# Value pages of a hybrid decoder step: sums of groups of four pages, on TensorE in column strips and on VectorE

## The reference

```python
t_inv = inverse(eye + L)                 # L: strictly lower part of (k*beta) k^T * decay
u = t_inv @ v_beta
w = t_inv @ (k_beta * exp(g))
def step(S, xs):
    v_new = u_c - w_c @ S
    o = q_c @ S + attn_c @ v_new
    S = S * exp(gl) + k_c^T @ v_new
```

```python
v_past = v_pool[page_table].reshape(db, past, HA, DVA)      # 8 x 16 pages of 128 x (4 heads x 128)
a = p[:, :, 0] - lam * p[:, :, 1]                           # weights, one for each position and head
out = einsum('bhqk,bkhe->bqhe', a, v)
```

## Time and profile before

| | us |
|---|---|
| median of 3 runs (lowest to highest) | 2703.61 (2703.09 to 2705.79) |
| the profiled execution | 2701.74 |
| its span, which the rows below divide | 2699.8 |
| TensorE busy, over the span | 2622.1 (97%) |
| VectorE busy, over the span | 1614.7 (60%) |
| ScalarE, GpSimd busy | 1142.6, 1346.6 |
| L1396, 360 of its operations | 106.9 |

### The profile page before, as it was taken

One profiled execution on the slowest core, in us unless ns is written; L12 is line 12 of the kernel. 1 busy time (PEld: TensorE's weight loads), 2 busy tenths in 40 slices (PEclk: granted clock), 3 DMA queues, 4 the chain that ended last, 5 costly groups with the idle time before them and its releaser, 6 DMA issues.

```text
span 2699.8 us, 46857 instructions
## 1 busy us (share of the span) xinstructions
PE 2622.1 (97%) x17069; PEld 2408.8 (89%) x17069; DVE 1614.7 (60%) x3290; ACT 1142.6 (42%) x1771; POOL 1346.6 (50%) x613
## 2 busy tenths in 40 slices
PE   8999999978899999999999999999999999999998
PEld 5886666667766899999999999999999999999998
DVE  4227768889977343333337885378863788634323
ACT  2228739954423343334333434344343433444433
POOL 0210015610000666667666676676766767666663
PEclk9999999988899999999999999999999999999999
DMA  5220057634585444444444444454444444444553
GB/s 182 68 95 9 17 173 222 195 103 133 155 251 156 134 143 141 137 139 138 139 140 141 134 140 130 138 147 133 140 132 144 132 142 140 134 132 141 149 156 95
DMA packets 457194, 369.01 MB, mean 137 GB/s; under 512 B 15501, under 2 KB 400114, under 8 KB 456732
## 3 DMA queue, kind: packets, MB, share of 16 engines
q1 hardware_dynamic: 444846, 347.05, 43.6%
q0 software_dynamic: 2992, 12.26, 1.5%
q10 hardware_dynamic: 9174, 7.22, 0.9%
HBM read 351.17 MB, written 17.14 MB: 136 GB/s over the span
## 4 chain that ended last, share of the span: by engine, by line
PE 67%; DVE 2%; ACT 1%; issue 1%; DMA 0%; SPq 0%; POOL 0%; DVEq 0%; ACTq 0%
PE bank L2867 21%; PE bank L2869 21%; PE bank L2868 21%; PE bank L2359 3%; DVE tmp L2735 1%; DVE bank L3448 1%; ACT tmp L2727 1%; DMA big<-in_cache_attn_v 0%; PE bank L2743 0%; PE bank L3651 0%; PE bank L2379 0%; SPq L1128 0%; DVE hh L3405 0%; DVE hl L3406 0%; PE bank L1759 0%
## 5 line engine op out<-in xcount | busy, mean ns | idle before, releaser
L3326 POOL TENSOR_TENSOR wl<-wring,wh 128x1024 fp32r<-128x1024 f32 x466 | 1137.4, 2456 | 589.3 <-ACT wh L3083 588.9
L2867 PE MATMUL bank<-xh,wh 128*128 128x344 f32 x2688 | 862.2, 321 | 0.3 <-POOL wl L3326 0.3
L2869 PE MATMUL bank<-xh,wl 128*128 128x344 f32 x2688 | 858.4, 319 | 0.0
L2868 PE MATMUL bank<-xl,wh 128*128 128x344 f32 x2688 | 856.8, 319 | 0.0
L3083 ACT ACTIVATE wh<-wring 128x1024 fp32r<-128x1024 f32 x466 | 484.1, 1055 | 766.3 <-PE bank L2869 642.4
L2867 PEld LDWEIGHTS bank<-xh,wh 128*128 128x128 f32 x2688 | 505.6, 188 | 1.8 <-POOL wl L3326 0.6
L2868 PEld LDWEIGHTS bank<-xl,wh 128*128 128x128 f32 x2688 | 504.0, 188 | 1.2
L2869 PEld LDWEIGHTS bank<-xh,wl 128*128 128x128 f32 x2688 | 505.0, 188 | 0.0
L3404 DVE TENSOR_TENSOR bank<-bank,gates_tmp 128x344 f32<-128x344 f32 x132 | 69.1, 524 | 512.0 <-PE bank L2869 420.0
L3448 DVE SCALAR_TENSOR_TENSOR bank<-big,vec,bank 128x344 f32<-128x344 f32 (+1 forms) x696 | 354.5, 572 | 0.5
L2867 PE MATMUL bank<-hh,wh 128*128 128x344 f32 x1040 | 334.2, 321 | 3.2 <-DVE hl L3406 3.2
(11 more groups left out here) (441 smaller groups left out, 3182.9 us busy)
## 6 DMA issues: line engine op xcount, KB each, us to landing
wring<-in_ffn_w_down SPq DMA_DIRECT2D x132, 512.0 KB, 3.6
wring<-in_ffn_w_gate SPq DMA_DIRECT2D x131, 512.0 KB, 3.9
wring<-in_ffn_w_up SPq DMA_DIRECT2D x131, 512.0 KB, 3.9
wring<-in_conv_w_pw SPq DMA_DIRECT2D x72, 512.0 KB, 3.8
big<-in_cache_attn_k SPq DMA_DIRECT2D x128, 256.0 KB, 3.0
big<-in_cache_attn_v SPq DMA_DIRECT2D x128, 256.0 KB, 2.9
wring<-in_w_in SPq DMA_DIRECT2D x20, 512.0 KB, 4.0
park<-res_a SPq DMA_DIRECT2D x1, 4128.0 KB, 12.9
```

Of the source, the lines that this page charges most:

```text
L2867: pe.matmul(bank_out, h, mh, start=(n == 0), stop=False)
L2868: pe.matmul(bank_out, h, ml, start=False, stop=False)
L2869: mm = pe.matmul(bank_out, l, mh, start=False, stop=(n == len(terms) - 1))
L3326: pool.tensor_tensor(wl[s % 6][:, :], raw_w[s % WQ] if raw is None else raw, wh[s % 6][:, :].bitcast(F32), ALU.subtract).then_inc(w_cut, 1)
```

## The change

In each turn the 12 pages are now three groups of four.

- The first two groups go to TensorE (`page_group`). Four products of 128x32 weights by a whole page of 128x512 write to the four strips of 32 partitions of one PSUM bank (bank 5 for the first group, bank 6 for the second). Of the 32 weight columns, four are the heads' weights for that page; the others give rows that nothing reads. VectorE then copies or adds the bank to `strip_sum` in SBUF (`group_copy`, semaphore `group_in`).
- The third group stays on VectorE, pages 0 and 1 late in turn k, pages 2 and 3 early in turn k + 1. After the last turn two such pages follow.
- `page_column` adds, for the batches in the loop, four products of `strip_sum` with the columns of `fold`, which pick and sum the four strips.
- `keys_queries` goes ahead of `turn_values` on TensorE, and their marks in `set_at` change places.
- TensorE gets waits: ahead of the first group for the last VectorE page and for bank 5 (`attn_done`), ahead of the second for bank 6 (`k_scaled`), ahead of `values_new` and `outputs` for the group copies. Pages are still used in order, so a group waits for all pages before it.

The core of the diff:

```diff
+        def page_group(pe, g, n):
+            b, at = g * STRIPS // PG, g * STRIPS
+            pe.wait_ge(vpage_used, 8 + at)
...
+            for q in range(STRIPS):
+                pp, u = (at + q) % PG // 2, q % 2
+                w = aw_flat[:, (at + q) * H:(at + q) * H + 32]
+                mm = pe.matmul(bank[32 * q:32 * (q + 1), n, :], w, ring[:, pp % 4, u, :], start=True, stop=True)
+            mm.then_inc(vpage_used, STRIPS)
+
+        def group_copy(dve, g, n):
+            b = g * STRIPS // PG
+            dve.wait_ge(vpage_used, 8 + STRIPS * (g + 1))
+            d, src = strip_sum[b % 2].rearrange("p h e -> p (h e)"), bank[:, n, :]
+            if g == first_of(b, True):
...
+                dve.tensor_copy(d, src).then_inc(group_in, 1)
+            else:
+                dve.wait_ge(group_in, pe_groups(g))
+                dve.tensor_tensor(d, d, src, ALU.add).then_inc(group_in, 1)
...
             for h in range(H):
-                mm = pe.matmul(bank[:, n, h:h + 1], pacc[b][:, h, :], ones[:, 0:1], start=True, stop=True)
+                mm = pe.matmul(bank[:, n, h:h + 1], pacc[b][:, h, :], ones[:, 0:1], start=True, stop=not strips)
+                if strips:
+                    mm = pe.matmul(bank[:, n, h:h + 1], strip_sum[b % 2][:, h, :], fold[:, h:h + 1], start=False, stop=True)
...
                 left(k - 1, 3)
+                keys_queries(k)
                 turn_values(k)
-                keys_queries(k)
...
                 turn_keys(k)
+                if k < NB:
+                    pe.wait_ge(attn_done, k + 1)
+                else:
+                    pe.wait_ge(vn_copied, k - 1)
+                page_group(pe, 3 * (k - 1), 5)
                 left(k, 0)
...
+                pe.wait_ge(group_in, 2 * k - 1)
                 values_new(k - 1)
                 left(k, 2)
+                pe.wait_ge(group_in, 2 * k)
                 outputs(k - 1)
```

More of the change, by code:

```diff
@@ L1383, in page_sum @@
                 dve.wait_ge(page_in[pp % 4], b * 64 + (512 + 32 * (pp // 4 + 1)))
-            if g % PG == 0 and 2 <= b < 6:
+            first = g == STRIPS * first_of(b, False)
+            if first and 2 <= b < 6:
                 dve.wait_ge(samp_full, b - 1)
@@ L1392, in page_sum @@
                 w, d = aw_flat[:, at:at + 1], pacc[b][:, h, :]
-                if g % PG == 0:
+                if first:
                     last = dve.tensor_scalar(d, v, w, None, ALU.mult)
@@ L1610, in build, with on_pe, pe_groups, first_of @@
         samp_full, sacc_done = sem("samp_full"), sem("sacc_done")
-        PAGES = (0,) + 8 * (12,)
-        LATE = sum(PAGES)
+        STRIPS = 4
+        GROUPS = 3 * NB
+        LATE = STRIPS * GROUPS
         SAMPLE_AT = {2: 0, 4: 1, 5: 2, 6: 3, 8: 4}
-        KK, VT, QK, KT = 1, 2, 3, 4
+        group_in = sem("group_in")
+        strip_sum = [flat(16 * TT, H, P), flat(16 * TT + 512, H, P)]
+        def on_pe(g):
+            return g < GROUPS and g % 3 < 2
+        def pe_groups(g):
+            return sum(on_pe(n) for n in range(g))
+        def first_of(b, pe):
+            return next(g for g in range(b * PG // STRIPS, (b + 1) * PG // STRIPS) if on_pe(g) == pe)
+        KK, QK, VT, KT = 1, 2, 3, 4
         def set_at(c, what):
@@ L1813, in page_column @@
             pe.wait_ge(vpage_used, 8 + PG * (b + 1))
+            strips = pe_groups((b + 1) * PG // STRIPS) if b < LATE // PG else 0
+            if strips:
+                pe.wait_ge(group_in, strips)
             for h in range(H):
-                mm = pe.matmul(bank[:, n, h:h + 1], pacc[b][:, h, :], ones[:, 0:1], start=True, stop=True)
+                mm = pe.matmul(bank[:, n, h:h + 1], pacc[b][:, h, :], ones[:, 0:1], start=True, stop=not strips)
+                if strips:
+                    mm = pe.matmul(bank[:, n, h:h + 1], strip_sum[b % 2][:, h, :], fold[:, h:h + 1], start=False, stop=True)
             mm.then_inc(samp_full, 1)
+        def page_group(pe, g, n):
[3 more added lines that the diff above has]
+                pp, u = (at + q) % PG // 2, q % 2
+                if u == 0:
+                    pe.wait_ge(page_in[pp % 4], b * 64 + 512 + 32 * (pp // 4 + 1))
+            for q in range(STRIPS):
+                pp, u = (at + q) % PG // 2, q % 2
+                w = aw_flat[:, (at + q) * H:(at + q) * H + 32]
[6 more added lines that the diff above has]
+            if g == first_of(b, True):
+                if b >= 2:
+                    dve.wait_ge(samp_full, b - 1)
+                else:
+                    dve.wait_ge(bias_io, 64)
+                dve.tensor_copy(d, src).then_inc(group_in, 1)
+            else:
+                dve.wait_ge(group_in, pe_groups(g))
+                dve.tensor_tensor(d, d, src, ALU.add).then_inc(group_in, 1)
         def page_column_in(dve, b, n):
@@ L2032, in chunk_pe @@
                     on_sum(pe, 2, ON_BANK[2])
+                    pe.wait_ge(oc_copied, k - 1)
+                else:
+                    pe.wait_ge(k_scaled, k + 1)
+                page_group(pe, 3 * (k - 1) + 1, 6)
                 right_turned(k - 1, 5)
@@ L2174, in chunk_dve @@
         def chunk_dve(dve, step):
-            def page(k, n):
-                if n < PAGES[k]:
-                    page_sum(dve, sum(PAGES[:k]) + n)
             def decays(c):
@@ L2331, in chunk_dve @@
                 join_turned(k, 2)
-                page(k, 11)
+                page(k, 1)
                 lower(k + 1)
-                page(k, 12)
                 if k in SAMPLE_AT:
                     page_column_in(dve, SAMPLE_AT[k], 2 * ((k + 1) % 2))
+            page(NB, 2)
+            page(NB, 3)
         vecf = vec[:].rearrange("p k v -> p (k v)")
```

20 lines of the change are left out of this document (9 added, 11 removed).

## The result

The changed kernel takes 2711.66 us (median of 10 runs, 2709.89 to 2717.63) against 2703.54 us (10 runs, 2701.22 to 2706.78) of the kernel before on the same chip: ratio 1.0031, 95% interval 1.0021 to 1.0040. It is slower by 8 us, where 2 us faster was forecast. The profiled execution took 2712.34 us, 2710.5 of them its span.

The account below looks back on a forecast made before the run. Inside a turn no engine was simply full: waits between TensorE and VectorE, then the falling clock, set it. -7.7 us at full clock plus 5.6 for clock falls gave -2.1, from 2703.6 to 2701.5 us; range 2692 to 2716.

Parts of the forecast that it names:

- Step 4: Ahead of the level-3 join: VectorE's page 2 adds 1.05 us, level-4 product 6.56 us after level 3, not 5.51.
- Step 6: New values to turn's end: turn of 23.4 us, or 24.9 with a column sum of 1.9 us on the path.
- Step 8: Granted clock early in the turn: falls in two of six turns, 2.5 us each, 0.6 in the last: +5.6 us.
- Step 7: Full-clock sum: six turns -5.6 us, last turn 19.3 against 20.5, first -0.3, after the loop -0.6; in all -7.7.
- Step 1: Strip products on TensorE: a group of four takes 1.05 us, upper bound 3.4, lower 0.85.
- the rival of serial strips: Both groups of each turn: strips run one after another, 2.35 us more for each of 16 groups, 2735 us; chance 0.13.
- Step 2: VectorE's work per turn: eight pages leave, two copies or adds come, giving 7 to 8 us of room.
- Step 3: Turn's start up to the key-state product, 4.43 us after level 3: moving the key-query products ahead gains nothing.
- Step 5: First group to new values: join waits of 1.23 and 1.36 us go, new values 0.83 us earlier.
- The rival of late pages: Second group's pages land late, costing a microsecond or two only at 728 to 745; near no change; chance 0.03.
- The rival "the clock falls in every turn": Clock falls at the wait for the level-3 join in every turn: +8.3 us, 2712 us; chance 0.12.

Follow-up runs that it names:

- filled: Changed kernel plus four unread 128x128 products on TensorE behind the key-state product in each turn but the last: 2706.24 us, 1.0011 of the kernel before.
- page_behind: Changed kernel with VectorE's page 2 moved back behind the level-3 join: 2704.09 us, 0.9998 of the kernel before.
- product_later: Changed kernel with GpSimd's product of the decayed queries held until VectorE has summed its four pages: 2706.89 us, 1.0009 of the kernel before.
- no_strip_sums: Changed kernel without the four products that add the strip sums into a column sum: 2701.72 us, 0.9996 of the kernel before.
- queries_back: Changed kernel with the key-query products behind the turned values again: 2710.33 us, 1.0029 of the kernel before.
- spread: Changed kernel with VectorE's four pages moved, three ahead of the level-2 join, one behind the lower triangle: 2686.61 us, 0.9938 of the kernel before.
- spread_queries_back: Changed kernel with VectorE's pages moved to its idle places and key-query products behind the turned values again: 2686.59 us, 0.9938 of the kernel before.

## Why the prediction was wrong

The forecast was 2701.5 us, and 2711.66 came: inside the range of 2692 to 2716, with the wrong sign. By the forecast's steps turns 2 to 8 add up to 146.4 + 19.3 + 5.6 = 171.3 us; the profile has 181.14. Three steps failed: the size of the hole (4), the cost of a column sum (6) and, most of all, the number of the clock's falls (8). Of the 9.8 us between the two sums:

- **Step 4, the hole: 2 us of work, taken for 1.** The mechanism was right: page 2 ahead of the join holds up the level-4 product, with nothing to hide it. Its size, 1.05 us, came from a page that ran alone. This page runs beside GpSimd's product, 2.11 us instead of 1.14. With the hole at t = 7.48 instead of 6.56, and steps 5 and 6 half a microsecond better than worked out, a full-clock turn without a column sum is 23.86 us (`filled`) and not 23.4.
- **Step 6, the column sum.** 1.9 us were worked out for its own time and 1.5 for the turn; it costs the turn 1.78 (25.64 less 23.86). With the point above, the six turns at full clock are 4 x 25.64 + 2 x 23.86 = 150.3 us and not 146.4: **3.9 us**.
- **Step 8, the clock: the larger part.** Falls were expected in two of six turns, 5.0 us; they came in five, once twice as long and once with a second fall behind the column sum. The six turns took 159.6 us, 9.3 more than at full clock: **4.3 us**. The number was the guess between rivals that the text called it. The price of 2.5 us was that of a turn with twice the low clock (2.6 measured, in turns 4 and 5); a single fall cost 1.4 to 1.5, so two such turns would have been 2.9 us and not 5.0, and the number was off by more than the 4.3 us show. The place was nearly right: t = 6.2 to 9.0, in the hole or up to 1.5 us behind it, where 6 to 7 was forecast. That the hole is to blame is shown from two sides: `filled` and `page_behind` have waits of 1.0 to 1.6 us there too, but more work between them, and no fall; in `product_later` the wait is 0.9 us with nothing put in, and the falls stay.
- **Step 7, the last turn.** 19.3 us at full clock plus 0.6 were expected, 21.58 came: **1.7 us**. The outputs wait for the second group's add, as was forecast, for 1.56 us, and run at half clock behind it. `product_later` has the same wait and a last turn of 19.89 us at full clock (below), and so has `no_strip_sums` with its wait of 2.46. So the 19.3 was 0.6 too low, and the clock took 1.7 instead of 0.6: with the last turn it explains 5.4 of the 9.8 us.

```profile
772.39 0.79 PE L2024 MATMUL bank<-res_b,state 128*128 128x128 f32 x2 [1.56 <-DVE big L1867]
```

```profile
755.23:775.12 19.89, 16.87 (x198) 12.61 (x195) 14.71 (x46) 8.90 (x29) 0.00 (x0) 1.00 0.78 235
```

Outside turns 2 to 8 the forecast had 0.9 us less (-0.3 for the first turn, -0.6 behind the loop), and the profiles have 2.1 more. Of that, 2.7 us came ahead of the loop's first product, where nothing was changed.

What was right. *Step 1:* a group holds TensorE for 0.99 us, expected 1.05; the instructions are 0.6 us long and overlap in the strips. The Trainium skill (TensorE: Matmul & The Clock Gate, Part 3: Packing small matmuls) let one estimate 1.4 us for four; the trace decides for less, and the rival of serial strips (2735) is out. *Step 2:* VectorE is relieved by 6 to 8 us a turn (7 to 8 expected). *Step 3:* the moved key-query products bring nothing (`queries_back`), and for the stated reason: once the seeds come early (`spread`), they bring 0.6 us. *Step 5:* the waits for the late joins are gone. The rival of late pages is true only where it was placed, in turn 7, and at its price of a microsecond or two: there the second group waits 1.01 us for its pages (at 746.96) and VectorE 3.27 us (at 753.72).

The rival "the clock falls in every turn" said 2712, and that is what came, though only in part by its terms: it took the full-clock turns 3.9 us too low and the falls too high. It was given 0.12. The row ahead of the fall in the earlier trace rows had TensorE busy for 2.54 of 3.40 us; the forecast hole was emptier than that, which spoke for the rival. But in the turn at 619 us of the kernel before a stretch as long had 2.05 and no fall, so the rows did not decide:

```profile
633.00:636.40 3.40, 2.05 (x55) 1.83 (x54) 3.22 (x11) 1.52 (x8) 0.42 (x1) 1.00 0.50 157
```

**What stays open.** Whether the clock falls at the sixteen one-column instructions is not settled turn by turn: in `page_behind` turn 5 has them and no fall, in `filled` turn 2, and in `spread_queries_back` three of four turns. The place in which they come relative to earlier light stretches was not varied by itself. And no kernel had all pages on VectorE and spread in this way, so how much of the 28.6 us the groups on TensorE give, and how much the places of the pages, is not separated.

## What to carry to other kernels

Work that is taken off a busy engine is worth what the other engines then wait less, so the order of what remains must be made anew: with the same pages on each engine a turn without a column sum took 23.9 us at full clock with a page ahead of a join (in `filled`), and 20.7 with the pages where VectorE had idle time. Price a moved instruction by the row of that very instruction with its neighbours on all engines, not by the shortest row of its kind. And where the granted clock falls in part of a stretch, count the cost of a hole or of a chain of one-column products twice, for its length and for what runs at half clock behind it; adding work can then be a gain (`filled`).

## What the runs showed of the hardware

- Four fp32 products of 128x32 weights by 128x512 values, one in each column strip, hold TensorE for 0.99 us together (639.32 to 640.31). Four ordinary ones in a row would hold it for 3.4, an estimate from the one at 361.16.
- VectorE operations with two SBUF operands took longer beside a GpSimd product from SBUF: four that take 1.14 us alone took 2.11 beside one of 1.26 us that had started 0.08 us earlier, and 1.75 where it had started 0.45 us earlier. The time went to the first of the four, which ended 0.15 us behind GpSimd's product; with that product held back (`product_later`) the four took 1.11. The Trainium skill (SBUF — State Buffer, Who interferes with whom) has this as a lock on a shared pair of ports that the later instruction waits for in full; by that rule the page would take the 1.18 us to the product's end at 629.21 and its own 1.14, 2.3 us, and 1.95 in the kernel before. The rows agree to 0.2 us, being shorter by that in both cases.
- The granted clock fell to 0.50, which is 1.2 GHz, with no wait of TensorE ahead of it, at or behind sixteen one-column instructions of 1.88 us in all, in four of four turns of `spread`; with eight of them (1.05 us) it stayed at 1.00 (2.4 GHz) in turns 2 to 7. In `spread_queries_back`, whose TensorE also waits 0.80 us early in the turn, it fell in one of the four turns with sixteen.
- It also fell where one set of products of 1.13 us stood between waits of 1.14 and 0.91 us (`product_later`, five of six turns), and stayed where 2.8 us of products stood between waits of 1.15 and 1.63 us (`page_behind`, turn 5).
